# Gate/up units of four FFNs as seven half-width products, with one weight sum made by transfers

## The chip, the core and the metric

The kernel runs on one core of one Trainium2 chip. The metric is the device time of one execution in microseconds (us): from three runs of the kernel before, the median is 2486.27 us (2479.25 to 2486.68). TensorE is called PE, VectorE DVE, ScalarE ACT, GpSimd POOL; SP is the engine that issues most of the loads.

## What is computed

Two transformer blocks over 512 positions of width 1024, batch 1, all in 32-bit floats: pooling with grid attention, an mLSTM, HGRN2 beside stick-breaking attention, a cross-attention to a memory of 256 rows, and four feed-forward parts. The change touches only the four feed-forward parts:

```python
FFN_HIDDEN = 2816
def swiglu(h, w1, w3, w2):                # ffn0 and ffn1
    return (jax.nn.silu(h @ w1) * (h @ w3)) @ w2
def swiglu_2(h, w_gu, w_down):            # ffn2 and ffn3
    gu = h @ w_gu
    gate, up = jnp.split(gu, 2, axis=-1)
    return (jax.nn.silu(gate) * up) @ w_down
# x = x + g2 * swiglu(h, w1, w3, w2)      or      x = x + 0.5 * swiglu_2(rmsnorm(x), w_gu, w_down)
```

## The kernel before

**Layout.** Activations stand with features on the 128 partitions: `x`, `h_hi`, `h_lo` are 8 chunks (KC) of 128 features x 512 positions. Weights come from HBM as `stream`, one unit of 128 x 2048 floats (1 MB) after the other, into `raw`, which has two slots (unit m uses slot m % 2).

**Three passes.** To keep the precision of 32 bits, each operand is split in a rounded high part and the rest: for weights ACT writes `w_hi` (`split_hi`, L214) and DVE `w_lo` (`split_lo`, L218). Each product is three matmuls: hi x hi, hi x lo, lo x hi (`three_passes`, L231 to L233).

**An FFN** (`FeedForward`) has 22 gate/up units (FB) and 11 down units. A gate/up unit holds 128 columns of the gate and 128 of the up weights, each over 8 chunks: 2 x 8 x 3 = 48 matmuls of 512 columns, into two PSUM banks. ACT takes the silu of the gate bank (L717), or of the copy that DVE scaled first (L747, L749, then L714) where the norm is deferred (ffn2 and ffn3: the matmuls begin on x times gain, and the row factors `inv_rows` are applied to the results). DVE multiplies by the up half (L754), ACT writes `g_hi` (L719) and DVE `g_lo` (L756). Then `split_next_hi` and `split_next_lo` split the weights two units ahead. The 22 chunks of g stay in SBUF. A down unit is 2 chunks of g x 8 output blocks x 3 passes, again 48 matmuls of 512 columns; all eight banks accumulate over the 11 units, and DVE adds the result to x (L786) as the banks of the last unit end.

**Queues.** Each engine runs its own list in order; waits are on semaphores. SP loads unit m as soon as the split of unit m - 2 is done (`lo_split`, L2796). POOL issues most loads of the conditioning weights (`load_ada`, L2788, 48 units of 1 MB in all, 13 of them by SP), of which DVE adds up 8 in the gate/up units of ffn0 and 16 in its down units (`Conditioning.add_unit`, L326). In ffn0, the norm before it and ffn1's are of the plain kind (`Norm`), in which DVE scales x chunk by chunk, ACT writes `h_hi` and DVE `h_lo`.

## Time and profile before

| | |
|---|---|
| median of 3 runs | 2486.27 us (2479.25 to 2486.68) |
| profiled execution, span from first to last instruction | 2481.9 us |
| four FFNs, matmuls of 512 columns | 4 x 33 x 48 = 6336 of 12256 |
| HBM read | 263.90 MB, 107 GB/s over the span |

Durations below come from the one profiled execution. Its span of 2481.9 us is within the three runs and 4.4 us under their median. In the profile a line like L218 is that of a helper, so one line stands for all its uses; the shapes tell them apart. Matmuls are pipelined: the duration of one is longer than the distance from one to the next, and it is the distance that counts. Where a row tells of idle time before a group of instructions, the releaser is the instruction that ended the wait.

### The profile page before, as it was taken

The page shows a single profiled execution, that of the slowest core. Times are in us where ns is not written, and L with a number is a line of the kernel's source. Part 1 is how long each engine was busy: PE and PEld are TensorE (multiplying, and loading weights), DVE is VectorE, ACT ScalarE, POOL GpSimd, SP SyncE. Part 2 cuts the span into 40 slices and gives each one's busy share as a digit, 9 for nine tenths or more (in the row PEclk, how much of TensorE's full clock was granted, in tenths as well). Part 3 has the DMA queues.
Part 4 walks back from the last instruction along what each step waited for, and adds up shares of the span by engine and source line. Part 5 has one row for each costly group of instructions (what it writes and reads, how often), then busy time and mean ns, then how long its engine had stood idle before and what let it go on. Part 6 is the DMA issues. An engine that isn't in the chain of part 4 may idle for free.

```text
span 2481.9 us, 30237 instructions
## 1 busy us (share of the span) xinstructions
PE 2416.7 (97%) x12256; PEld 2022.5 (81%) x12256; DVE 1238.3 (50%) x1449; ACT 902.1 (36%) x1215; POOL 70.3 (3%) x81
## 2 busy tenths in 40 slices
PE   7989999999999999999999999999999999999998
PEld 6658888888799778888878888879989877888886
DVE  6677543356746543332254442346678545444423
ACT  3353333313344333332143332244556544333311
POOL 0210000000003000000000000000000000000000
PEclk9999999999999999999999999999999999999999
DMA  8116522364233122222222222221212212222221
GB/s 341 73 63 243 186 102 101 139 239 164 87 123 91 68 84 86 101 101 100 87 85 101 98 88 102 102 98 69 85 52 79 75 68 85 85 101 101 88 100 67
DMA packets 40549, 267.34 MB, mean 108 GB/s; under 512 B 4394, under 2 KB 5674, under 8 KB 9490
## 3 DMA queue, kind: packets, MB, share of 16 engines
q1 hardware_dynamic: 31248, 219.87, 24.6%
q0 software_dynamic: 5840, 40.37, 4.2%
q10 hardware_dynamic: 3378, 5.91, 0.9%
q8 instruction: 61, 1.00, 0.2%
q14 instruction: 22, 0.18, 0.0%
HBM read 263.90 MB, written 2.24 MB: 107 GB/s over the span
## 4 chain that ended last, share of the span: by engine, by line
PE 89%; DVE 6%; ACT 3%; issue 1%; DMA 0%; DVEq 0%; SPq 0%; ACTq 0%
PE bank L231 26%; PE bank L233 26%; PE bank L232 26%; DVE w_lo L218 1%; PE bank L2160 1%; ACT w_hi L214 1%; PE bank L2256 1%; PE bank L334 1%; PE bank L2243 1%; PE bank L1868 1%; DVE work L461 1%; DVE work L445 1%; PE bank L2231 1%; PE bank L1864 1%; ACT work L438 1%
## 5 line engine op out<-in xcount | busy, mean ns | idle before, releaser
L231 PE MATMUL bank<-h_hi,w_hi 128*128 128x512 f32 x1800 | 711.1, 395 | 5.3 <-DVE w_lo L218 2.0
L233 PE MATMUL bank<-h_hi,w_lo 128*128 128x512 f32 x1800 | 703.3, 391 | 0.0
L232 PE MATMUL bank<-h_lo,w_hi 128*128 128x512 f32 x1800 | 703.3, 391 | 0.0
L218 DVE TENSOR_TENSOR w_lo<-raw,w_hi 128x2048 fp32r<-128x2048 f32 x192 | 439.9, 2291 | 477.6 <-ACT w_hi L214 477.6
L214 ACT ACTIVATE w_hi<-raw 128x2048 fp32r<-128x2048 f32 x192 | 366.3, 1908 | 413.1 <-PE bank L233 409.6
L231 PEld LDWEIGHTS bank<-h_hi,w_hi 128*128 128x128 f32 x1800 | 339.5, 189 | 82.0 <-issue 6.7
L233 PEld LDWEIGHTS bank<-h_hi,w_lo 128*128 128x128 f32 x1800 | 339.4, 189 | 71.8
L232 PEld LDWEIGHTS bank<-h_lo,w_hi 128*128 128x128 f32 x1800 | 339.7, 189 | 70.6 <-issue 1.4
L233 PE MATMUL bank<-g_hi,w_lo 128*128 (+1 forms) x704 | 273.9, 389 | 0.0
L231 PE MATMUL bank<-g_hi,w_hi 128*128 (+1 forms) x704 | 273.9, 389 | 0.0
L232 PE MATMUL bank<-g_lo,w_hi 128*128 (+1 forms) x704 | 273.9, 389 | 0.0
L231 PEld LDWEIGHTS bank<-g_hi,w_hi 128*128 128x128 f32 x704 | 132.1, 188 | 27.5
L232 PEld LDWEIGHTS bank<-g_lo,w_hi 128*128 128x128 f32 x704 | 132.1, 188 | 27.5
L233 PEld LDWEIGHTS bank<-g_hi,w_lo 128*128 128x128 f32 x704 | 132.1, 188 | 27.3
L754 DVE TENSOR_TENSOR work<-work,bank 128x512 f32<-128x512 f32 x44 | 30.2, 688 | 212.5 <-ACT work L717 212.5
L231 PE MATMUL bank<-w_hi,h_hi 128*128 128x256 f32 x448 | 130.4, 291 | 2.0 <-DVE w_lo L218 2.0
L232 PE MATMUL bank<-w_lo,h_hi 128*128 128x256 f32 x448 | 127.3, 284 | 0.0
L233 PE MATMUL bank<-w_hi,h_lo 128*128 128x256 f32 x448 | 127.2, 284 | 0.0
L717 ACT ACTIVATE work<-bank 128x512 f32<-128x512 f32 x44 | 26.3, 598 | 277.0 <-PE bank L233 274.9
L714 ACT ACTIVATE work<-work 128x512 f32<-128x512 f32 x44 | 27.8, 632 | 262.6 <-DVE work L747 262.6
L747 DVE TENSOR_TENSOR work<-bank,inv_rows 128x512 f32<-128x512 f32 x44 | 30.4, 692 | 165.8 <-PE bank L233 160.5
L756 DVE TENSOR_TENSOR g_lo<-work,g_hi 128x512 f32 (+1 forms) x88 | 61.0, 693 | 79.0 <-ACT g_hi L719 79.0
(331 smaller groups left out, 2816.9 us busy)
## 6 DMA issues: line engine op xcount, KB each, us to landing
raw<-stream SPq DMA_DIRECT2D x192, 1024.0 KB, 4.8
work<-stream POOLq DMA_DIRECT2D x19, 1024.0 KB, 6.5
h_plain<-stream POOLq DMA_DIRECT2D x16, 1024.0 KB, 5.4
work<-stream SPq DMA_DIRECT2D x13, 1024.0 KB, 12.3
work<-mlstm_rows ACTq DMA_DIRECT2D x8, 512.0 KB, 4.8
x<-xT SPq DMA_DIRECT2D x1, 2048.0 KB, 10.5
outT<-work SPq DMA_DIRECT2D x8, 256.0 KB, 2.3
work<-mlstm_rows ACTq DMA_DIRECT2D x8, 192.0 KB
```

Source lines behind the costliest of these rows:

```text
L214: nc.scalar.activation(w_hi[:, slot(m), :], raw[:, slot(m), :], ACT.Copy).then_inc(hi_split, 1)
L218: nc.vector.tensor_tensor(w_lo[:, slot(m), :], raw[:, slot(m), :], w_hi[:, slot(m), :], ALU.subtract).then_inc(lo_split, 1)
L231: nc.tensor.matmul(out, stationary[0], moving[0], start=first, stop=False)
L232: nc.tensor.matmul(out, stationary[0], moving[1], start=False, stop=False)
L233: return nc.tensor.matmul(out, stationary[1], moving[0], start=False, stop=last)
L334: last = nc.tensor.matmul(bank[:, self.banks[a], 16 * q + b:16 * q + b + 1], self.acc[a][:, b * P:b * P + P], ones[:, 0:1], start=True, st ...
L438: nc.scalar.activation(self.sq[:, k, :], x[:, k, :], ACT.Square).then_inc(sq_done, 1)
L714: nc.scalar.activation(self.silu[:, r, :], self.silu[:, r, :], ACT.Silu).then_inc(silu_done, 1)
L717: nc.scalar.activation(self.silu[:, r, :], bank[:, b, :], ACT.Silu).then_inc(silu_done, 1)
L747: nc.vector.tensor_tensor(self.silu[:, r, :], bank[:, b, :], inv_rows[:, :], ALU.mult).then_inc(rows_scaled, 1)
L754: nc.vector.tensor_tensor(self.gu[:, r, :], self.silu[:, r, :], up, ALU.mult).then_inc(gated, 1)
L756: nc.vector.tensor_tensor(g_lo[:, bass.ds(2 * i + r, 1), :], self.gu[:, r:r + 1, :], g_hi[:, bass.ds(2 * i + r, 1), :], ALU.subtract).then ...
```

## The change

Of the 22 gate/up units of each FFN the first 4 (`FFN_WHOLE`) stay as they are. The other 18 (`FAST`) compute the same 2 x 2 block product with seven products instead of eight. The unit's output is seen as gate and up rows x first and second 256 positions, the inner dimension as even and odd chunks. A product is then 4 chunks x 3 passes of 256 columns, and there are seven: 84 matmuls of 256 columns in place of 48 of 512.

- **Weights.** The host stores a fast unit as four parts of 512 columns: a12, a11, a22 and a fourth (`parts` in `ffn_units`). Four more blocks are sums of them. s3 and s1 are made by a transfer of POOL that accumulates parts 2 and 3 on a copy of parts 1 and 2 (`mixes`, 0.25 MB + 0.25 MB). s2 = s3 + a22 is made by DVE (`make_further`). s4, the sum of all four, is made by POOL: a plain transfer of part 0 into `further`, then a transfer that accumulates s2 on it (`add_further`).
- **Activations.** POOL forms five differences of quarters of h (`gpsimd`), in a deferred stage after eight multiplications by the gain; ACT and DVE split the result (`hidden_high`, `hidden_low`).
- **Results.** ACT copies the first product (`keep_first`), DVE makes three additions (`add_first`) and a last one (`add_last`); then silu and gating (`apply`, `gate_chunk`).
- **Splits.** A fast unit is split in three pieces instead of one: three plain blocks (`whole_high`, `whole_low`), two mixes, two further blocks. The chunks of g are kept whole and split in pairs beside the down units (`pair_high`, `pair_low`).
- **Loads.** SP issues three transfers for a fast unit (parts 0 and 1, part 3, parts 1 and 2). The loops over units on all engines are written out. The down weights wait until `further`, which lies in the fourth quarter of both `raw` slots, is free.
- Some semaphores are merged (`set_loaded`, `act_prepared`, `dve_prepared`), and the rings of the conditioning loads in ffn0 move.

The core of the diff:

```diff
+FFN_WHOLE = 4
+            mixes = [area(4096, UNIT // 2), area(5120, UNIT // 2)]
+            further = raw[:, :, 3 * (UNIT // 4):]
+            def load(self, sp, m):
+                q, r, s = self.QUARTER, m - self.fast(0), slot(m)
+                sp.wait_ge(lo_split, m - 1)
+                src = stream[place_of(m), :, :]
+                sp.dma_start(raw[:, s, 0:2 * q], src[:, 0:2 * q]).then_inc(landed[s], 16)
+                sp.dma_start(raw[:, s, 2 * q:3 * q], src[:, 3 * q:]).then_inc(landed[s], 16)
+                sp.wait_ge(part_lo, self.hidden_lows(2) if r < 2 else self.part_low("mixes", r - 2))
+                sp.dma_start(self.mixes[s], src[:, q:3 * q]).then_inc(landed[s], 16)
+            def add_parts(self, pool, r):
+                q, s = self.QUARTER, slot(self.fast(r))
+                pool.wait_ge(landed[s], landings(self.fast(r)))
+                pool.dma_start(self.mixes[s], stream[place_of(self.fast(r)), :, 2 * q:], accum_op=ALU.add).then_inc(
+                    mixed_in[s], 16)
+            def add_further(self, pool, r):
+                if r:
+                    pool.wait_ge(part_lo, self.part_low("further", r - 1))
+                else:
+                    pool.wait_ge(lo_split, self.fast(0))
+                pool.dma_start(self.further[:, 1, :], stream[place_of(self.fast(r)), :, 0:self.QUARTER]).then_inc(further_in, 16)
+                pool.wait_ge(further_in, 32 * (self.w0 + r) + 16)
+                pool.wait_ge(part_lo, self.part_low("s2", r))
+                pool.dma_start(self.further[:, 1, :], self.further[:, 0, :], accum_op=ALU.add).then_inc(further_in, 16)
+            def gpsimd(self, pool):
...
+                for i, (out, one, two) in enumerate(((b11, b12, b11), (b12, b22, b12), (b21, b22, b21), (b22, b11, b22),
+                                                     (b21, b21, b11))):
+                    nc.gpsimd.tensor_tensor(out, one, two, ALU.subtract).then_inc(hidden_sums, 1)
+                    pool.wait_ge(hidden_sums, self.sums_base + self.sums_first + i + 1)
...
+                self.add_parts(pool, 0)
+                for r in range(FAST):
+                    if r + 1 < FAST:
+                        self.add_parts(pool, r + 1)
+                    self.add_further(pool, r)
+            def make_further(self, dve, r):
+                nc.vector.tensor_tensor(s2, s3, a22, ALU.add).then_inc(part_lo, 1)
+            def further_high(self, act, r):
+                act.wait_ge(further_in, 32 * (self.w0 + r + 1))
+                act.wait_ge(unit_used, self.fast(r))
+                nc.scalar.activation(out, self.further, ACT.Copy).then_inc(part_hi, 1)
+            # ACT, fast units
+                for r in range(FAST):
+                    self.further_high(act, r)
+                    if r:
+                        self.apply(act, r - 1)
+                    if r + 1 < FAST:
+                        self.whole_high(act, r + 1)
+                    self.keep_first(act, r)
+                    if r + 1 < FAST:
+                        self.mixes_high(act, r + 1)
+            # DVE, fast units
+                for r in range(FAST):
+                    self.further_low(dve, r)
+                    if r:
+                        self.add_last(dve, r - 1)
+                    if r + 1 < FAST:
+                        self.make_further(dve, r + 1)
+                    if r:
+                        self.gate_chunk(dve, r - 1)
+                    if r + 1 < FAST:
+                        self.whole_low(dve, r + 1)
+                        self.mixes_low(dve, r + 1)
...
+                    self.add_first(dve, r)
+                    if self.ada and r and r % 2 == 0 and r < 16:
+                        conditioning.add_unit(dve, 3 * KC + r // 2)
+            # PE, fast units: 3, 2 and 2 products of 4 chunks x 3 passes x 256 columns
+            def plain_products(self, pe, r):
+                pe.wait_ge(lo_split, self.fast(r) + 1)
...
+            def mixes_products(self, pe, r):
+                pe.wait_ge(part_lo, self.part_low("mixes", r))
...
+            def further_products(self, pe, r):
+                pe.wait_ge(part_lo, self.part_low("further", r))
...
+                    if m == ffn.md or m == ffn.md + 1:
+                        sp.wait_ge(part_lo, ffn.part_low("further", FAST - 1))
```

## Rows read from the trace of the kernel before

**Rows 1.** The page: busy time by engine, and the chain that ended last.
```profile
PE 2416.7 (97%) x12256; PEld 2022.5 (81%) x12256; DVE 1238.3 (50%) x1449; ACT 902.1 (36%) x1215; POOL 70.3 (3%) x81
PE 89%; DVE 6%; ACT 3%; issue 1%; DMA 0%; DVEq 0%; SPq 0%; ACTq 0%
```

**Rows 2.** Windows: stretches inside the FFNs; the last beside POOL's conditioning loads.
```profile
core 0: us, PE busy (x) PEld busy (x) DVE busy (x) ACT busy (x) POOL busy (x), PEclk, DMA share, GB/s
...
338.00:468.00 130.00, 130.00 (x585) 108.00 (x584) 42.05 (x37) 42.44 (x41) 0.00 (x0) 0.99 0.26 93
905.00:1035.00 130.00, 130.00 (x575) 107.66 (x574) 43.67 (x36) 44.16 (x42) 0.00 (x0) 1.00 0.27 96
1295.00:1425.00 130.00, 130.00 (x576) 107.63 (x575) 59.60 (x60) 44.56 (x42) 0.00 (x0) 1.00 0.28 96
...
1120.00:1150.00 30.00, 30.00 (x134) 24.85 (x133) 8.26 (x5) 6.05 (x6) 0.00 (x0) 1.00 0.30 105
540.00:600.00 60.00, 60.00 (x266) 49.67 (x266) 36.33 (x17) 11.50 (x6) 3.70 (x7) 1.00 0.62 235
```

**Rows 3.** Groups by line, 1295 to 1425 us, DVE and ACT (x12 is 12 units).
```profile
L218 DVE TENSOR_TENSOR w_lo<-raw,w_hi 128x2048 fp32r<-128x2048 f32 x12 | 27.5, 2293 | 11.7 <-ACT w_hi L214 11.7
L747 DVE TENSOR_TENSOR work<-bank,inv_rows 128x512 f32<-128x512 f32 x12 | 8.3, 692 | 46.5 <-PE bank L233 46.5
...
L214 ACT ACTIVATE w_hi<-raw 128x2048 fp32r<-128x2048 f32 x12 | 22.8, 1900 | 0.0
...
L719 ACT ACTIVATE g_hi<-work 128x512 f32 x12 | 7.6, 633 | 10.6 <-DVE work L754 10.6
```

**Rows 4.** Timeline of DVE in the down stage of ffn1 (start us, us, instruction).
```profile
1194.48 2.29 DVE L218 TENSOR_TENSOR w_lo<-raw,w_hi 128x2048 fp32r<-128x2048 f32 x1 [8.64 <-ACT w_hi L214]
1205.30 2.29 DVE L218 TENSOR_TENSOR w_lo<-raw,w_hi 128x2048 fp32r<-128x2048 f32 x1 [8.53 <-ACT w_hi L214]
1216.24 2.29 DVE L218 TENSOR_TENSOR w_lo<-raw,w_hi 128x2048 fp32r<-128x2048 f32 x1 [8.64 <-ACT w_hi L214]
1227.06 2.29 DVE L218 TENSOR_TENSOR w_lo<-raw,w_hi 128x2048 fp32r<-128x2048 f32 x1 [8.53 <-ACT w_hi L214]
1237.94 2.29 DVE L218 TENSOR_TENSOR w_lo<-raw,w_hi 128x2048 fp32r<-128x2048 f32 x1 [8.59 <-ACT w_hi L214]
```

**Rows 5.** Timeline of ACT in the odd input stage, where units are 256-column matmuls.
```profile
701.06 1.21 ACT L1481 ACTIVATE work<-bank 128x256 f32<-128x256 f32 x4 [8.51 <-PE bank L233]
...
712.58 1.21 ACT L1481 ACTIVATE work<-bank 128x256 f32<-128x256 f32 x4 [2.02 <-PE bank L233]
```

**Rows 6.** Windows: the odd input stage around those units.
```profile
680.00:720.00 40.00, 40.00 (x337) 40.00 (x336) 22.10 (x30) 15.49 (x25) 5.13 (x4) 1.00 0.39 125
```

**Rows 7.** Groups of the whole span: fused DVE kinds, gate update of 512, conditioning of 2048.
```profile
L326 DVE SCALAR_TENSOR_TENSOR work<-work,cond 128x2048 f32<-128x2048 f32 x28 | 65.8, 2348 | 9.5 <-DMA work<-stream 8.6
...
L786 DVE SCALAR_TENSOR_TENSOR x<-bank,par,x 128x512 f32<-128x512 f32 x16 | 11.8, 748 | 9.2 <-PE bank L233 9.1
```

**Rows 8.** DMA issues (median us from issue to landing), and POOL's issues themselves.
```profile
raw<-stream SPq DMA_DIRECT2D x192, 1024.0 KB, 4.8
...
outT<-work SPq DMA_DIRECT2D x8, 256.0 KB, 2.3
...
work<-mix_tables POOLq DMA_DIRECT2D x1, 768.0 KB, 4.6
...
L2788 POOL DMA_DIRECT2D work<-stream x19: 527/527/599, 51.0 to 315.8; - x19
```

**Rows 9.** POOL's additions: duration min/median/max ns, and their group.
```profile
L1581 POOL TENSOR_TENSOR work<-work,tab x16: 1262/1296/3071, 694.7 to 798.8; 128x512 f32<-128x512 f32 x16
...
L1581 POOL TENSOR_TENSOR work<-work,tab 128x512 f32<-128x512 f32 x16 | 24.7, 1564 | 194.9 <-DMA work<-mlstm_rows 194.9
```

**Rows 10.** Windows: the tail of ffn1 and the start of ffn2.
```profile
1240.00:1265.00 25.00, 22.95 (x100) 18.11 (x99) 18.46 (x27) 13.86 (x21) 0.00 (x0) 0.93 0.21 75
```

More of the change, by code:

```diff
@@ new lines, in whole_high, with whole_low @@
+            def whole_high(self, act, r):
+                m = self.fast(r)
+                act.wait_ge(landed[slot(m)], landings(m))
+                if r:
+                    act.wait_ge(products, self.product_done(4, r - 1))
+                else:
+                    act.wait_ge(unit_used, m - 1)
+                nc.scalar.activation(self.weights(0, 3)[0], raw[:, slot(m), 0:3 * self.QUARTER], ACT.Copy).then_inc(hi_split, 1)
+            def whole_low(self, dve, r):
+                m = self.fast(r)
+                dve.wait_ge(hi_split, m + 1)
+                hi, lo = self.weights(0, 3)
+                nc.vector.tensor_tensor(lo, raw[:, slot(m), 0:3 * self.QUARTER], hi, ALU.subtract).then_inc(lo_split, 1)
@@ L839, in rows @@
-                def rows(d, i, first=False, end=False):
-                    m = self.md + d
+                    if j == 0 and self.norm.deferred:
+                        self.norm.spread_row(pe)
+                pe.wait_ge(part_lo, self.hidden_lows(2))
+                for r in range(FAST):
+                    self.plain_products(pe, r)
+                    self.mixes_products(pe, r)
+                    self.further_products(pe, r)
+                    if self.ada and r == 15:
+                        conditioning.sum_rows(pe, 3)
```

542 lines of the change are left out of this document (385 added, 157 removed).

## The prediction

> **What bounds the kernel now.** I read the busy table and the chain that ended last first: TensorE (PE) is busy 97% of the span and carries 89% of the chain; VectorE (DVE) is busy 50%, ScalarE (ACT) 36%, GpSimd (POOL) 3% [rows 1]. Then the stretches inside the gate/up stages of the four FFNs: PE is busy for the whole of each, DVE for 42 to 60 of 130 us, the DMA engines for 0.26 to 0.28 of their time at 93 to 96 GB/s, and the granted clock is 0.99 to 1.00, so TensorE runs at its upper level of 2.4 GHz [rows 2]. Nothing but matmul time limits these stages: DVE waits for PE's banks and for ACT (46.5 us before L747 in one stretch) [rows 3]. So removed matmul work is worth its full time, until something else takes longer per unit. A unit, gate/up or down, is 48 matmuls of 512 columns. The DVE splits of five successive weights of a down stage start 10.82 to 10.94 us apart (43.46 us for four, mean 10.87): 226 ns a matmul [rows 4].
>
> **What a fast unit costs on PE.** Of the 22 gate/up units of each FFN, 18 become seven products of 4 chunks x 3 passes: 84 matmuls of 256 columns. If time went by columns alone, that would be 84/96. The row for 256 columns is in the odd input stage: a unit of 96 such matmuls is evacuated at 701.06 and the next at 712.58, 11.52 us, 120 ns each [rows 5]; there the weight load is busy in all of 40.00 us, so the load, not the column count, sets that pace [rows 6]. 84 x 0.120 = 10.08 us against 10.87: 0.79 us saved per unit, 72 units, 57 us. The ceiling is therefore 2481.9 - 57 = 2425 us.
> The Trainium skill (TensorE: Matmul & The Clock Gate, Back-to-back issue gap) gives a warm isolated gap of columns/2.4 + 2.5 ns. By it a unit would go from 10.36 to 9.17 us and 72 units would save 86 us. The rows show a smaller gain and decide.
>
> **DVE and ACT in a fast unit.** DVE takes 0.69 us for 512 columns and 2.29 for 2048 [rows 3], hence 0.16 + 1.04 per 1000 columns: 0.42 at 256, 1.22 at 1024, 1.76 at 1536. Per unit: low parts 1.76 + 1.22 + 1.22; `make_further`, two of `add_first` and `add_last` 4 x 0.69; the third add 0.42; the gating 0.75 (the fused kind, [rows 7]). Sum 8.1, and 8.8 where the norm is deferred (one more 0.69). It was 3.7 and 5.0. That is under 10.08, but no longer hidden by half an engine of slack: the order of the queue now matters. In ffn0 nine conditioning additions of 2.35 [rows 7] add 1.2 per unit: 9.3. ACT: 0.63 at 512 and 1.90 at 2048 [rows 3] give 1.06 + 1.48 + 1.06 + 0.63 + 0.4 = 4.6, no bound.
>
> **The transfers, the step that decides.** The stream per unit was one 1 MB load. Now it is 1.25 MB by SP (parts 0-1, part 3, then parts 1-2 again into `mixes`), and three POOL transfers: 0.5 MB accumulated into `mixes`, 0.25 MB plain into `further`, and 0.25 MB accumulated there from SBUF. The last two form a chain that goes through every unit, since `further` is one buffer: `further_low`(r-1) on DVE, POOL issues the plain one, waits until it has landed, issues the accumulating one, ACT `further_high`, DVE `further_low`(r). Prices: a plain 0.25 MB takes 2.3 us from issue to landing, 1 MB 4.8, hence 1.5 + 3.3 per MB; POOL's 0.75 MB took 4.6 where this gives 4.0, so 0.5 more on POOL (its issue alone is 0.53) [rows 8]. Plain into `further`: 2.8.
> No row shows an accumulating transfer. Below, it costs what a plain one of its size does; I see no reason for a saving under that. It must read its destination as well as its source and write the sum, so the nearest row is a transfer of twice its bytes, which I take: 0.25 MB for 1.5 + 0.5 + 1.65 = 3.6 us, and 0.5 MB of it occupies the queue for 3.3 us. Above, I take three times the bytes.
> The chain then is 2.8 + 3.6 + 1.06 + 1.22 + 0.3 for the hand-overs (five at about 0.06) = 9.0 us. Alone it would fit under 10.08. But POOL issues `add_parts`(r+1), 0.5 MB accumulating, just before the plain transfer of `add_further`(r), in the same queue. Its source `mixes` is free only after `mixes_low`(r-1), its reload takes about 3.2 us and shares the engines, so it goes out about when `further_low`(r-1) ends, and the plain transfer stands behind it. Of its 3.3 us of service I count 2.8 on the chain: period 11.8 us. With a price like a plain one it is 8.2 + 1.4 = 9.6, under PE's 10.08; with three times the bytes 9.9 + 4.2 = 14.1.
> Why PE must follow: on DVE `whole_low`(r+1) is queued behind `further_low`(r), `add_last`, `make_further` and the gating (4.6 to 5.3 us after it), and `plain_products`(r+1) waits for it; `further_products`(r) waits for the chain itself. The engines move 2.25 MB, as I price it the work of 3 MB, in 11.8 us, 254 GB/s; 235 GB/s took a share of 0.62 [rows 2], so bandwidth is not exceeded, but transfers will meet each other.
> The Trainium skill (DMA: Bandwidth & Descriptors, Anatomy of one DMA) gives 2.0 us + bytes/436e3 per POOL transfer: 2.6 us for 0.25 MB, near the row's. By it the chain with both transfers at that price is 7.8 us and the change would reach PE's floor. It says nothing of an accumulating transfer, and the sum keeps the rows.
>
> **Entry and exit.** Entry: POOL forms five differences of 1024 columns per partition; its 512-column rows last 1.27 to 1.56 us [rows 9], so 12.5 to 15.6. They start when h is complete, some 10.5 us after its first chunk (two fused DVE steps of 0.75 for each of seven more, [rows 7]); then come 5 us of ACT and 4 of DVE: 32 to 35 us. The silu of unit 1 is queued behind them on ACT, and unit 3, due at 32.6 or later, needs it. 0 to 3 us each; I take 1, four times: 4. In deferred stages POOL's eight gains also run beside DVE's x updates at the tail of the stage before, where PE already idles 2.05 of 25 us [rows 10]; 0 to 3 us, in the same 4. Exit: the down weights of the first pair can load only after the last `further_low`, since `further` lies in `raw`: 4.8 + 1.90 + 2.29 [rows 3, 8] = 9.0 us to the first down matmul. The last unit's products cover about 5.5 of it: 3.5 lost, four times 14. Before there was no such wait: PE is busy for the 30 us around the turn [rows 2]. In the down stage g is split in pairs: 1.06 ACT, 2.4 DVE beside 10.87 of PE, hidden by PE, at most 2 x 2.35 more in ffn0 (9.4 in all). The renamed semaphores and SP's unrolled loads cost nothing: they stand off PE's path.
>
> **Sum.** -57 (matmuls), + 72 x (11.8 - 10.08) = +124 (chain), -16 (in the first two to three units of each stage the chain has a lead, about 4 us each), +4, +14: 2481.9 + 69 = 2551. The median lies 4 us above the profiled span: 2555 us, 2.8% slower.
>
> **The rivals, and how the numbers follow.** The time is 2447 + 72 x (period - 10.08), less up to 16 for the lead.
> A, the forecast: the chain through `further` sets a period of 11 to 13 us. For it: the in-order queues as written, and two landings one after the other per unit. Chance 0.50, 2505 to 2625.
> B, the accumulating transfer costs like a plain one: the chain stays under 10.08, only entry and exit remain: 2481.9 - 57 + 18 + 4 = 2447, faster. It decides at a period of 10.6: above it the chain has eaten 72 x 0.5 = 36 us of the 57, entry and exit the rest. For it: fixed latency (1.5 of 2.3) is most of a small transfer, and a source in SBUF may be quicker. Chance 0.20.
> C, in between, 1.25 to 1.5 times: period 10.4 to 11.1, 2470 to 2512, within 1%. Chance 0.17.
> D, the accumulating transfers are three times or more, or the stalls (2 us and more per unit) also lower TensorE's clock: where PE idled at the tail above, the granted clock was 0.93 [rows 10]. Period 13 and up, 2640 and more. Chance 0.10.
> E, DVE becomes the bound instead: its 8.8 us grow if POOL and DVE hold each other up (one POOL row of 512 columns took 3.07 us against 1.27 [rows 9]). From 10.08 on it decides; at 10.6 the result is about 2485. Chance 0.03.
> Range: 2445 to 2640 leaves out most of D and little else. This kernel's measurement tells about 0.3% (7 us) from no change. Faster: B and a fifth of C, 0.23; same: 0.07; slower: 0.70.
>
> **What would show it.** PE idle of 1.5 to 2 us before the matmuls of `plain_products` and `further_products`, ended by DVE's `w_lo` writes; ACT's `further_high` waiting for a DMA; POOL waiting most of its time between the two transfers. Right if their starts lie 11 to 13 us apart, accumulating landings take 3 to 4 us (5 for 0.5 MB), and DVE is idle 2 us or more per unit. Wrong if the period is 10.1 and PE has no gaps (B), if DVE is busy without a gap (E), or if a 256-column matmul with weights as the stationary side is not 120 ns: at 113 ns the ceiling falls by 42 us, but the chain would hide that.

## The result, and the profile after

The changed kernel takes 2718.18 us (median of 4 runs, 2713.82 to 2724.46) against 2486.47 us for the kernel before on the same chip: a ratio of 1.0949 (95% interval 1.0931 to 1.0967; the two medians alone give 1.0932). The forecast was 2555, with a range up to 2640: right in its direction, but the loss is 232 us where 69 were expected.

The page of the changed kernel answers to rows 1 (busy time, queues, chain) and rows 8 (landings).

```profile
span 2716.4 us, 35297 instructions
PE 2452.1 (90%) x14848; PEld 2170.9 (80%) x14848; DVE 1612.4 (59%) x1913; ACT 989.8 (36%) x1369; POOL 327.7 (12%) x333
...
q0 software_dynamic: 32336, 115.88, 18.5%
...
PE 53%; DMA 23%; DVE 11%; ACT 7%; issue 4%; POOL 2%; SPq 0%; ACTq 0%; DVEq 0%; POOLq 0%
...
work<-stream SPq DMA_DIRECT2D x72, 512.0 KB, 6.1
work<-stream POOLq DMA_DIRECT2D x72, 512.0 KB, 5.7
...
raw<-stream POOLq DMA_DIRECT2D x72, 256.0 KB, 4.1
raw<-raw POOLq DMA_DIRECT2D x72, 256.0 KB, 4.6
```

PE fell from 97% busy to 90%, and from 89% of the chain to 53%; transfers, absent from the chain before, carry 23%. The last four lines are, in order, SP's reload of `mixes`, POOL's accumulation on it, the plain transfer into `further` and the accumulating one. L240, L960 and the other line numbers from here on are those of the changed kernel (L240 is a matmul, L960 is the difference in `further_low`, L922 that in `whole_low`, L937 that in `mixes_low`).

The waits (engine and line, what ended the wait, us in total, times, longest):

```profile
ACT w_hi L955 <- DMA raw<-raw: 479.3, 71, 12.2
POOL work L817 <- DMA work<-stream: 431.0, 72, 21.6
...
POOL raw L829 <- DMA raw<-stream: 311.5, 71, 7.6
...
PE bank L240 <- DVE w_lo L960: 133.2, 40, 6.4
...
PE bank L240 <- DVE w_lo L922: 32.8, 30, 2.0
```

ACT waits for the accumulated sum in 71 of 72 units. PE waits behind it in only 40, about every second one, but then 3.3 us in the mean.

Windows answer to rows 2: four long ones inside the fast units of ffn0 to ffn3, three short ones in ffn2 ahead of them, and last the turn from gate/up to down units in ffn1.

```profile
core 0: us, PE busy (x) PEld busy (x) DVE busy (x) ACT busy (x) POOL busy (x), PEclk, DMA share, GB/s
...
1500.00:1515.00 15.00, 13.61 (x114) 13.41 (x112) 7.89 (x10) 3.84 (x5) 3.16 (x4) 1.00 0.72 207
1515.00:1523.00 8.00, 5.39 (x33) 5.10 (x34) 6.72 (x8) 3.66 (x5) 1.44 (x2) 0.79 0.58 120
...
1541.00:1547.00 6.00, 4.40 (x24) 4.24 (x24) 4.87 (x6) 3.39 (x5) 1.16 (x2) 0.72 0.52 117
...
290.00:490.00 200.00, 158.76 (x1180) 154.63 (x1178) 120.53 (x130) 60.81 (x71) 34.98 (x47) 0.90 0.71 190
990.00:1200.00 210.00, 173.28 (x1221) 165.97 (x1220) 110.97 (x131) 62.94 (x76) 34.03 (x44) 0.91 0.68 169
1440.00:1640.00 200.00, 169.77 (x1284) 166.41 (x1283) 126.71 (x150) 65.50 (x76) 34.57 (x45) 0.93 0.70 181
2360.00:2560.00 200.00, 161.44 (x1227) 158.38 (x1228) 126.66 (x151) 65.50 (x76) 34.54 (x45) 0.93 0.69 173
...
1255.00:1270.00 15.00, 10.54 (x37) 8.35 (x36) 9.06 (x9) 5.29 (x4) 0.00 (x0) 0.77 0.38 129
```

Where the kernel before had the clock at 0.99 to 1.00 and the DMA engines at 0.26 to 0.28, the clock is now 0.90 to 0.93 and the engines are at 0.68 to 0.71. The loss of clock is not spread evenly: it is 1.00 in a stretch without a gap, and 0.72 to 0.79 in the short stretches in which PE has just stood idle for some 3 us. A closer look at one such place, the first matmul behind a wait and the 3 us after it:

```profile
1490.92 0.57 PE L240 MATMUL bank<-t_hi_tile,w_hi 128*128 128x256 f32 x1 [3.47 <-DVE w_lo L960]
```

```profile
1491.00:1494.00 3.00, 3.00 (x14) 3.00 (x15) 2.45 (x4) 1.78 (x2) 0.57 (x1) 0.50 0.75 179
```

The granted clock is 0.50 there, the lower level of 1.2 GHz, and the matmuls start 0.21 us apart; from 1494.45 on they start 0.12 us apart again.

**Where the 232 us lie.** Each FFN is taken from the start of DVE's last run of x updates before it (for ffn2, which follows ffn1 directly, from ffn1's first update) to its own first update. The four FFNs took 1448.1 us before and 1680.7 after: all of the loss. By stages (timelines of PE and DVE, the four summed; before, the 18 units are 18 x 10.87, rows 4):

| us, four FFNs | before | after | difference |
|---|---|---|---|
| entry and the 4 whole units | 215.2 | 229.6 | +14.4 |
| 18 fast units and the wait behind them | 782.7 | 990.9 | +208.2 |
| down units | 450.0 | 460.2 | +10.2 |

Of the 990.9 us, 72 x 10.08 = 726 are matmuls at the forecast pace, 166 are PE's waits for L960 and L922 (133.2 + 32.8), 17.7 the four waits at the exits (6.9 and 10.8). What is left, 81 us, is time above the forecast pace. The clock windows account for most of it: at a mean clock of about 0.92, the 807 us in which PE works take 807 x (1 - 0.92) = 65 us more than at 1.00. PE's timelines say it directly: 608 of the 6048 matmuls start 0.21 or 0.22 us after the one before, the pace of the lower level, and cost 57 us more than at 0.120. Some 12 us more lie at the 75 waits, where idle time counts only from the end of the last matmul, and 4 are 32 small matmuls of the conditioning, which the table's column for the kernel before has in its first row.

**One turn of the loop.** The timelines of SP, POOL and DVE in ffn2 (start us, us, instruction, idle time before it and what ended it) show what sets the pace:

```profile
1523.02 0.37 SPq L811 DMA_DIRECT2D work<-stream  x1
```

```profile
1517.00 0.57 POOL L826 DMA_DIRECT2D raw<-stream  x1 [2.87 <-DVE w_lo L960]
1520.55 0.87 POOL L829 DMA_DIRECT2D raw<-raw  x1 [2.99 <-DMA raw<-stream]
1528.74 0.88 POOL L817 DMA_DIRECT2D work<-stream  x1 [7.32 <-DMA work<-stream]
1529.28 0.91 POOL L826 DMA_DIRECT2D raw<-stream  x1
1535.50 0.86 POOL L829 DMA_DIRECT2D raw<-raw  x1 [5.32 <-DMA raw<-stream]
```

```profile
1499.48 1.22 DVE L960 TENSOR_TENSOR w_lo<-raw,w_hi 128x1024 fp32r<-128x1024 f32 x1 [0.55 <-ACT w_hi L955]
...
1515.47 1.22 DVE L960 TENSOR_TENSOR w_lo<-raw,w_hi 128x1024 fp32r<-128x1024 f32 x1 [6.70 <-ACT w_hi L955]
...
1521.77 1.22 DVE L937 TENSOR_TENSOR w_lo<-work,w_hi 128x1024 fp32r<-128x1024 f32 x1
...
1525.21 1.23 DVE L960 TENSOR_TENSOR w_lo<-raw,w_hi 128x1024 fp32r<-128x1024 f32 x1 [0.44 <-ACT w_hi L955]
...
1541.32 1.22 DVE L960 TENSOR_TENSOR w_lo<-raw,w_hi 128x1024 fp32r<-128x1024 f32 x1 [6.82 <-ACT w_hi L955]
```

L960 starts 16.0 us after the last time, then 9.7, then 16.1: not every unit is slow, every second one is. From 1515.47: `whole_low` and `mixes_low` stand behind `further_low` in DVE's queue, so L937 ends only at 1522.99; that frees `mixes`, and SP starts its reload at 1523.02, 7.55 us after L960 began; POOL, next in its queue `add_parts` of that later unit (L817), waits until the reload has landed, to 1528.74 (5.72); only then does it issue the plain transfer of `add_further` (L826), whose buffer had been free since 1526.4; that one shares the engines with the 0.5 MB just issued and lands after 6.2 us (1535.50); the accumulating transfer, ACT and the hand-overs take 5.8. The sum is 7.55 + 5.72 + 0.54 + 6.22 + 5.82 = 25.85 us, for two units: 12.9 each. The means of the 17 steps in ffn2 and ffn3 are 12.8 and 13.0. The short step between is the chain through the one buffer without anything in its way: L960 at 1515.47, L826 at 1517.00, L829 at 1520.55, L960 again at 1525.21, 9.7 us where the forecast had 9.0.

### The profile page after: what moved, and what is told of

It is laid out like the page before. It is cut to its first block, busy times and chain, and to the rows that moved or that the text cites. A ratio compares the mean times of both kernels' runs of the same rounds, so it can differ in the third digit from the quotient of the medians.

```text
span 2716.4 us, 35297 instructions
## 1 busy us (share of the span) xinstructions
PE 2452.1 (90%) x14848; PEld 2170.9 (80%) x14848; DVE 1612.4 (59%) x1913; ACT 989.8 (36%) x1369; POOL 327.7 (12%) x333
## 3 DMA queue, kind: packets, MB, share of 16 engines
q0 software_dynamic: 32336, 115.88, 18.5%
## 4 chain that ended last, share of the span: by engine, by line
PE 53%; DMA 23%; DVE 11%; ACT 7%; issue 4%; POOL 2%; SPq 0%; ACTq 0%; DVEq 0%; POOLq 0%
PE bank L240 14%; PE bank L241 14%; PE bank L242 14%; DMA raw<-stream 8%; DMA work<-stream 7%; DMA raw<-raw 7%; ACT w_hi L916 2%; DVE w_lo L922 1%; ACT w_hi L955 1%; DVE w_lo L937 1%; POOL work L846 1%; DVE w_lo L227 1%; PE bank L343 1%; ACT w_hi L223 1%; PE bank L2554 1%
## 5 line engine op out<-in xcount | busy, mean ns | idle before, releaser
L240 PE MATMUL bank<-h_hi,w_hi 128*128 128x256 f32 (+1 forms) x1512 | 528.7, 350 | 44.9 <-DVE w_lo L922 32.8
L241 PE MATMUL bank<-h_lo,w_hi 128*128 128x256 f32 (+1 forms) x1512 | 515.0, 341 | 0.0
L242 PE MATMUL bank<-h_hi,w_lo 128*128 128x256 f32 (+1 forms) x1512 | 513.4, 340 | 0.0
L240 PE MATMUL bank<-t_hi_tile,w_hi 128*128 128x256 f32 x1152 | 343.4, 298 | 133.4 <-DVE w_lo L960 133.2
L240 PEld LDWEIGHTS bank<-h_hi,w_hi 128*128 128x128 f32 x1512 | 306.3, 203 | 85.7 <-DVE w_lo L922 39.7
L227 DVE TENSOR_TENSOR w_lo<-raw,w_hi 128x2048 fp32r<-128x2048 f32 x120 | 279.4, 2328 | 147.5 <-ACT w_hi L223 147.5
L240 PEld LDWEIGHTS bank<-t_hi_tile,w_hi 128*128 128x128 f32 x1152 | 232.2, 202 | 141.9 <-DVE w_lo L960 141.7
L242 PE MATMUL bank<-t_hi_tile,w_lo 128*128 128x256 f32 x1152 | 338.4, 294 | 0.0
L241 PE MATMUL bank<-t_lo_tile,w_hi 128*128 128x256 f32 x1152 | 338.1, 294 | 0.0
L240 PE MATMUL bank<-g_hi,w_hi 128*128 128x512 f32 x704 | 278.5, 396 | 18.1 <-DVE w_lo L227 10.8
L241 PE MATMUL bank<-g_lo,w_hi 128*128 128x512 f32 x704 | 277.1, 394 | 0.0
L242 PE MATMUL bank<-g_hi,w_lo 128*128 128x512 f32 x704 | 277.0, 393 | 0.0
L960 DVE TENSOR_TENSOR w_lo<-raw,w_hi 128x1024 fp32r<-128x1024 f32 x72 | 88.2, 1225 | 299.1 <-ACT w_hi L955 298.8
L242 PEld LDWEIGHTS bank<-t_hi_tile,w_lo 128*128 128x128 f32 x1152 | 233.7, 203 | 0.0
L240 PEld LDWEIGHTS bank<-g_hi,w_hi 128*128 128x128 f32 x704 | 134.3, 191 | 47.9 <-DVE w_lo L227 11.4
```

The costliest lines, as they stand in the source:

```text
L227: nc.vector.tensor_tensor(w_lo[:, slot(m), :], raw[:, slot(m), :], w_hi[:, slot(m), :], ALU.subtract).then_inc(lo_split, 1)
L240: nc.tensor.matmul(out, stationary[0], moving[0], start=first, stop=False)
L241: nc.tensor.matmul(out, stationary[0], moving[1], start=False, stop=False)
L242: return nc.tensor.matmul(out, stationary[1], moving[0], start=False, stop=last)
L960: nc.vector.tensor_tensor(lo, self.further, hi, ALU.subtract).then_inc(part_lo, 1)
```

## The experiments

Line numbers are those of each kernel; L960 and L976 are `further_low`.

### The sum of four blocks by DVE

```diff
                 nc.vector.tensor_tensor(s2, s3, a22, ALU.add).then_inc(part_lo, 1)
+                dve.wait_ge(part_lo, self.part_low("s2", r))
+                nc.vector.tensor_tensor(self.further[:, 1, :], s2, raw[:, s, 0:q], ALU.add).then_inc(part_lo, 1)
...
-                    self.add_further(pool, r)
```

> One part undone: the sum of all four blocks is a DVE addition of 512 columns again (0.69 us a unit), POOL's plain and accumulating transfers through the buffer further are gone, the accumulation into mixes stays. Theory Q (the queue theory: units are paced by the chain of landings through further, lengthened by POOL's order, in which the plain transfer stands behind the accumulation for the next unit; the starts of the low part of further alternate between 9.8 and 16 us, 12.9 on the mean in ffn2): the alternation goes, the period falls to 10.1 to 11 us, total 2470 to 2540 us. Rival V (DVE's in-order queue paces): 0.69 us more on DVE per unit, the period stays at 13 or rises, total 2700 to 2770 us. Rival B (the DMA engines are short of time, share 0.70): 0.5 of 2.25 MB less per unit, the period falls by a fifth, to 10.5 to 11.5, but the landings of mixes stay at 6 us.

2500.89 us, ratio 1.0071 (1.0053 to 1.0088). One addition of 0.69 us on DVE in place of the two transfers wins back 217 of the 232 us. Starts of `further_low` (here L961) in ffn1:

```profile
1025.46 1.22 DVE L961 TENSOR_TENSOR w_lo<-raw,w_hi 128x1024 fp32r<-128x1024 f32 x1
...
1035.54 1.22 DVE L961 TENSOR_TENSOR w_lo<-raw,w_hi 128x1024 fp32r<-128x1024 f32 x1
```

They are 10.08 us apart, the forecast's floor for PE, 84 x 0.120. So the pace of 120 ns for 256 columns [rows 5] carried over to weights of another shape, and in ffn1 the rest of the change, accumulating `mixes` included, fits under it (mean 10.1). In ffn2 and ffn3 the starts scatter (7.9 to 13.4 us) round means of 10.3 and 10.2, and in all DVE waits 28 times, 71.9 us, for an accumulation into `mixes`; only a part of that reaches PE. That the kernel still does not gain has other places. PE waits 15.2 us for `whole_low` and 19.9 for the splits of whole weights (L227), and ffn0 takes 384.2 us against 369.6 before.

### POOL issues the further sums first

```diff
                 for r in range(FAST):
+                    self.add_further(pool, r)
                     if r + 1 < FAST:
                         self.add_parts(pool, r + 1)
-                    self.add_further(pool, r)
```

> Same work, one order changed: POOL issues both transfers of further for unit r before the accumulation into mixes for unit r+1. Theory Q: the plain transfer is no longer behind the 0.5 MB accumulation, it lands 3.5 us after its issue every time (before 3.5 and 6.5 in turn), period 10.8 to 11.8, total 2560 to 2640 us. Rivals V and B: DVE's work and the bytes are the same, total stays within 15 us of 2718.

2669.69 us, ratio 1.0755 (1.0725 to 1.0786), 48 us less than the change, between the two ranges that I had given. The period is now irregular (9.5 to 17 us in ffn1 to ffn3), and the landings of the transfers for `mixes` are longer: 9.3 and 9.8 us instead of 6.1 and 5.7. That they now meet the chain through `further` is my explanation; no run shows it. The order costs something, but it is not the whole.

### Both accumulating transfers made plain

This kernel moves the same bytes and leaves the sums out.

```diff
-                pool.dma_start(self.mixes[s], stream[place_of(self.fast(r)), :, 2 * q:], accum_op=ALU.add).then_inc(
+                pool.dma_start(self.mixes[s], stream[place_of(self.fast(r)), :, 2 * q:]).then_inc(
...
-                pool.dma_start(self.further[:, 1, :], self.further[:, 0, :], accum_op=ALU.add).then_inc(further_in, 16)
+                pool.dma_start(self.further[:, 1, :], self.further[:, 0, :]).then_inc(further_in, 16)
```

> Both accumulating transfers are made plain ones of the same size and place, so the sums of the weight blocks are left out. It prices the accumulation. If an accumulation costs as much as twice its bytes (as I priced it), the landing of the 0.5 MB falls from 5.7 to about 4.2 us and that of the 0.25 MB from 4.6 to about 3.7; theory Q: 2.5 to 4 us less per two units, total 2580 to 2630 us. Rival B: share of the DMA engines falls from 0.70 to 0.55, period 10.5 or less, total under 2530. If the accumulation is nearly free: within 20 us of 2718.

2632.27 us, ratio 1.0581 (1.0557 to 1.0604): 86 us less, at the upper end of what I had expected. The bytes are the same (115.88 MB in the queue), the time is not:

```profile
q0 software_dynamic: 27728, 115.88, 12.8%
...
work<-stream POOLq DMA_DIRECT2D x72, 512.0 KB, 4.1
...
raw<-raw POOLq DMA_DIRECT2D x72, 256.0 KB, 2.8
```

The addition lengthens a landing of 512 KB from 4.1 to 5.7 us and one of 256 KB from 2.8 to 4.6. But 144 us of the loss (0.0581 x 2486) stay with plain copies, in the same pattern (in ffn2 9.2, then 15 to 16 us). A cheap accumulation would not have made the change pay: the loop alone loses.

### The sums of `mixes` by POOL's adder as well

On top of the first experiment, `add_parts` becomes two POOL additions of 512 columns; no accumulating transfer is left.

```diff
+                nc.gpsimd.tensor_tensor(m[:, 0:q], m[:, 0:q], m[:, q:], ALU.add).then_inc(mixed_in[s], 1)
+                pool.wait_ge(mixed_in[s], self.mixes_in(r) - 1)
+                nc.gpsimd.tensor_tensor(m[:, q:], m[:, q:], raw[:, s, 2 * q:3 * q], ALU.add).then_inc(mixed_in[s], 1)
```

> As e1_sum_on_dve, and the two sums of mixes are made by two POOL additions of 512 columns (about 1.3 to 1.6 us each) in place of the accumulating transfer: no accumulating transfer is left, 1.25 MB in three plain transfers per unit remain. Theory Q: period at PE's floor of 10.1 us but for DVE's queue, total 2445 to 2490 us. Rival V: no better than e1_sum_on_dve. If POOL and DVE hold each other up at SBUF, DVE's additions of 512 columns from SBUF get longer than 0.69 us and the total is over that of e1_sum_on_dve.

2530.73 us, ratio 1.0179 (1.0155 to 1.0202): 30 us slower than with the accumulating transfer and above the 2445 to 2490 that I had expected, with period 11.2 us in ffn2 and ffn3 (10.4 in ffn1). The timelines of POOL and DVE over a unit and the next show why:

```profile
1502.78 1.29 POOL L818 TENSOR_TENSOR work<-work 128x512 f32<-128x512 f32 x1 [8.93 <-DMA work<-stream]
1504.15 2.69 POOL L820 TENSOR_TENSOR work<-work,raw 128x512 f32<-128x512 f32 x1
```

```profile
1502.92 2.77 DVE L923 TENSOR_TENSOR w_lo<-raw,w_hi 128x1536 fp32r<-128x1536 f32 x1
1505.61 2.32 DVE L938 TENSOR_TENSOR w_lo<-work,w_hi 128x1024 fp32r<-128x1024 f32 x1
...
1514.24 1.76 DVE L923 TENSOR_TENSOR w_lo<-raw,w_hi 128x1536 fp32r<-128x1536 f32 x1
1515.92 1.22 DVE L938 TENSOR_TENSOR w_lo<-work,w_hi 128x1024 fp32r<-128x1024 f32 x1
```

While POOL adds (1502.8 to 1506.8), DVE's two differences take 1.0 and 1.1 us more than in the next unit, where POOL is silent; POOL's own second addition takes 2.69 where its first took 1.29. The four end in turn, POOL at 1504.07, DVE at 1505.69, POOL at 1506.84, DVE at 1507.93. DVE has no idle time from 1499.4 to 1514.1, longer than a whole unit, so what it loses to POOL here lengthens the period. This is the forecast's rival E, in the kernel where it decides. An accumulating transfer does have a use: it keeps such a sum off both engines.

### Two buffers for the further sums

In ffn1 to ffn3 `further` alternates between two buffers; the plain transfer waits for `further_low`(r-2) instead of (r-1).

```diff
+            def further(self, r):
+                return area(7168, 2, UNIT // 4) if r % 2 and not self.ada else self.shared
...
+            def before_further(self, eng, r):
+                back = r - (1 if self.ada else 2)
+                if back >= 0:
+                    eng.wait_ge(part_lo, self.part_low("further", back))
...
```

> The changed kernel, but the further sums of ffn1, ffn2 and ffn3 alternate between two buffers, so that the plain transfer of a unit waits for the difference two units back and not for the last one; GpSimd's order is that of the changed kernel, and so are all bytes. Chain theory (the time is set by a chain over two units that runs through the one buffer: difference, VectorE's queue, reload of the sums 6.1 us, its GpSimd accumulation, the plain transfer behind it 6.2, the accumulating one 3.6, ScalarE and VectorE 2.3): without the one buffer the chain opens, the starts of the difference L960 come every 10.1 to 11 us in ffn2 and ffn3 instead of 12.9 to 13.1, the clock there rises from 0.90 to above 0.95, and the time is 2718 less about 54 units of 2.3 us less some 45 us of clock: 2550, 2520 to 2590. Bandwidth theory (the DMA engines, 0.70 busy at 13 us per unit, would have to be 0.88 busy at 10.3, and landings grow before that): the period stays above 12 us, landings of the 256 KB accumulation grow beyond 5 us, and the time stays above 2660. Queue theory (VectorE's and GpSimd's order is what counts, not the buffer): the period hardly moves, with landings unchanged, above 2660 too.

2707.52 us, ratio 1.0902 (1.0873 to 1.0932). The chain theory as I had put it there fell: with the one buffer gone, 11 us come back, not 170. POOL and DVE in ffn2:

```profile
1493.06 0.88 POOL L836 DMA_DIRECT2D work<-stream  x1 [7.80 <-DMA work<-stream]
1494.37 0.57 POOL L843 DMA_DIRECT2D work<-stream  x1 [0.44 <-issue]
```

```profile
1479.50 1.23 DVE L976 TENSOR_TENSOR w_lo<-work,w_hi 128x1024 fp32r<-128x1024 f32 x1 [7.14 <-ACT w_hi L971]
1489.04 1.23 DVE L976 TENSOR_TENSOR w_lo<-raw,w_hi 128x1024 fp32r<-128x1024 f32 x1 [0.26 <-ACT w_hi L971]
1505.74 1.23 DVE L976 TENSOR_TENSOR w_lo<-work,w_hi 128x1024 fp32r<-128x1024 f32 x1 [7.39 <-ACT w_hi L971]
```

The plain transfer (L843) is free of its buffer, and is still issued only after POOL's 7.80 us for the reload; the long period is 16.7 us where it was 16.0 to 17.7. The turn of the loop above goes through two in-order queues, DVE's (`mixes_low` behind `further_low`) and POOL's (`add_further` behind `add_parts`), not through the buffer.

### Two buffers, and the further sums first

```diff
                 for r in range(FAST):
+                    self.add_further(pool, r)
                     if r + 1 < FAST:
                         self.add_parts(pool, r + 1)
-                    self.add_further(pool, r)
```

> The two buffers, and besides it GpSimd issues the further sums of a unit before the accumulation of the next unit's other sums, so that nothing of the further sums is queued behind the reload. Chain theory: the reload no longer stands in the path of the further sums at all; if the two buffers alone have opened the chain, this one changes little (within 30 us of the two-buffer run); if GpSimd's wait for the reload still holds the plain transfer, it is faster than that run by more than 30 us, near 2540. Bandwidth theory: both stay above 2660, and the landing of the reload or of the accumulation is longer than 6 us in the median.

2611.99 us, ratio 1.0515 (1.0497 to 1.0532): 96 us less than the two buffers alone, though not the 2540 that I had expected. Together the two edits bring 106 us, singly 48 and 11: each opens one of two paths into the same transfer. The period in ffn1 to ffn3 falls to 11.5 us in the mean, and the clock there rises to 0.97 to 0.98. The long step is now the path of `mixes`: its reload lands in 9.3 us and its accumulation in 9.2 (`DMA work<-stream` is 18% of the chain), and with 1.06 of ACT, 1.22 of DVE and 0.3 of hand-overs that is 21.1 us for a slot that comes round every two units: by this estimate 10.5 each before any wait in the engines' own queues, over PE's 10.08.

### The same, with plain copies

Here too the sums are left out.

```diff
-                pool.dma_start(self.mixes[s], stream[place_of(self.fast(r)), :, 2 * q:], accum_op=ALU.add).then_inc(
+                pool.dma_start(self.mixes[s], stream[place_of(self.fast(r)), :, 2 * q:]).then_inc(
...
-                pool.dma_start(self.further(r)[:, 1, :], self.further(r)[:, 0, :], accum_op=ALU.add).then_inc(further_in, 16)
+                pool.dma_start(self.further(r)[:, 1, :], self.further(r)[:, 0, :]).then_inc(further_in, 16)
```

> The kernel with two buffers and the further sums issued first, and both accumulating transfers made plain (as many bytes, but nothing is added: the sums of blocks are left out and the output is wrong for it). What remains between that kernel (2612) and the one with the sum on VectorE (2501) is 111 us. Theory: most of what remains is the price of the accumulating transfers on busy DMA engines (share 0.77 to 0.80 there, landings of 9 us); plain ones land in 4 to 6 us, the period falls from 11.5 to 10.3 to 10.8, and the time is 2560, 2530 to 2580. Rival (the bytes and the order of the queues are what remains, not the addition): the landings stay near 9 us, and the time stays above 2595.

2506.65 us, ratio 1.0095 (1.0074 to 1.0116): 105 us less, more than expected, and level with the sum on DVE. `further_low` starts every 10.1 us through ffn1 to ffn3, but for the first one or two steps; only ffn0, which has no second buffer here, is irregular (405.5 us against 384.2 with the sum on DVE). The queue and the same window in ffn1, first with the accumulating transfers, then with plain ones:

```profile
q0 software_dynamic: 32336, 115.88, 18.4%
...
990.00:1200.00 210.00, 187.08 (x1452) 181.97 (x1452) 132.07 (x156) 77.86 (x86) 41.07 (x53) 0.98 0.80 198
```

```profile
q0 software_dynamic: 27728, 115.88, 13.4%
...
990.00:1200.00 210.00, 206.38 (x1551) 198.49 (x1551) 141.87 (x158) 85.51 (x90) 23.92 (x45) 1.00 0.59 198
```

At the same 198 GB/s the engines are busy 0.80 of the time with accumulation and 0.59 without (the second window reaches 44 us into the down units, which end sooner there; over the fast units of ffn1 alone it is 0.79 at 199 GB/s against 0.66 at 221). In engine time: 18.4% of 2614.0 us is 481 us, 13.4% of 2504.4 is 336; the 145 us between them are 2.0 us of all 16 engines per unit for 0.79 MB accumulated. The same 0.79 MB plain take 336 / 115.88 x 0.79 = 2.3, so an accumulated byte costs 1.9 times a plain one. The same sum for the changed kernel and its plain copies gives 2.0.

So there are two prices, the order of the waits and the accumulation, and they nearly add up: 108 and 92 us singly, 212 together. The table gives the loss against the kernel before, from ratios times 2486 (hence 236 and not 232):

| | accumulating | plain copies |
|---|---|---|
| POOL's order of the change, one buffer | 236 | 144 |
| further sums first, one buffer | 188 | not run |
| order of the change, two buffers | 224 | not run |
| further sums first, two buffers | 128 | 24 |
| sum on DVE | 18 | |

### The differences of ffn2 late

On top of the first experiment, POOL's five differences of h in ffn2 wait for the scale of the norm.

```diff
+                    if not self.norm.squares_added:
+                        pool.wait_ge(inv_done, self.norm.n + 1)
```

> The kernel with the sum of all four blocks made by VectorE, and in ffn2's entry GpSimd's five differences wait until the norm's scale is ready. Theory of the shared memory port (VectorE's seven additions of squares took 13.5 us instead of 5.5 because GpSimd's 13.6 us of differences ran beside them): the additions take 5.5 to 7 us again, ffn2's entry is 5 to 8 us shorter, and the time is 2494, 2490 to 2498, against 2501. Rival (the additions wait on their inputs, or on ScalarE's squares): they take over 12 us again, and the time is 2500 or above, since the differences come later.

2497.45 us, ratio 1.0054 (1.0037 to 1.0071). DVE's seven additions of squares in ffn2's entry, first with the differences beside them, then without:

```profile
1264.33 13.52 DVE L454 TENSOR_TENSOR work<-work 128x512 f32<-128x512 f32 x7
```

```profile
1273.06 5.68 DVE L454 TENSOR_TENSOR work<-work 128x512 f32<-128x512 f32 x7
```

13.52 against 5.68 us (5.47 in the kernel before), and ffn2 takes 361.9 us instead of 370.7. Its entry, up to the first fast unit, is 58.7 us instead of 65.3 (56.5 in the kernel before). That settles most of the entry's loss in ffn2: two-input subtractions of POOL beside two-input additions of DVE. The total fell by only 3 us, inside the scatter of the two kernels' runs: ffn0, which the edit leaves alone, took 393.4 us in this profiled execution and 384.2 in the other.

### ffn0 as before

On top of the first experiment, ffn0 is the `FeedForward` of the kernel before: 22 whole units and its rings for the conditioning loads.

```diff
-            for name in ("ffn0", "ffn1", "ffn2", "ffn3"):
+            for name in ("ffn1", "ffn2", "ffn3"):
...
+        class WholeFeedForward:
```

> The kernel with the sum of all four blocks made by VectorE, with ffn0 computed as in the kernel before (22 whole units): one of the three edits of the combined kernel (2471). By the sum of stages ffn0 goes from 384 to 370 us and nothing else moves: 2487, 2482 to 2492. Rival (the combined kernel's gain came from the split load and the late differences, and ffn0 as it is costs nothing): 2496 to 2501.

2478.34 us, ratio 0.9972 (0.9959 to 0.9984): for the first time under the kernel before, and below the 2482 to 2492 that I had expected. By the profiled spans, ffn0 gives back 16.4 us (384.2 to 367.8) of 17.0; between the medians the gain is 22.6, since the profiled execution of the first experiment was its fastest. There the seven products save matmuls too, but DVE has the conditioning additions: in the first experiment it is busy 161.0 us of the 200 from 290 on, 9.0 us per unit at a mean period of 11.2. That this is what costs ffn0 its gain is a reading; no run shows it apart.

### ffn0 as before, late differences, down weights in two pieces

```diff
+                        for n in (m, m + 1):
+                            sp.dma_start(raw[:, slot(n), 0:c], stream[place_of(n), :, 0:c]).then_inc(landed[slot(n)], 16)
...
+                        for n in (m, m + 1):
+                            sp.dma_start(raw[:, slot(n), c:], stream[place_of(n), :, c:]).then_inc(landed[slot(n)], 16)
```

> The kernel of the run before with two more edits: ffn0 is computed as in the kernel before (22 whole units, no products of sums), and the down weights of the first pair are loaded in two pieces, three quarters before and one quarter after the last difference of the further sums. By the sum of stages: ffn0 went from 384 back to 370 us (-14); the port wait -7; the exits of three feed-forwards from about 4 us of idle TensorE to about 1 (-9): 2501 - 30 = 2471, 2460 to 2485, below the 2486 of the kernel before. Rival (each such stall only moves: a later load meets the next one): 2490 to 2505.

2471.12 us, ratio 0.9952 (0.9936 to 0.9969), 12 us under the kernel before: the fastest of the study. The total is as expected, but not for all of the expected reasons. PE's wait at ffn2's exit is 3.14 us with the split load and 3.14 without: it gained nothing there. The late differences cut PE's wait for the norm in ffn2 from 9.75 to 1.89 us, but 3.24 us of it come back at once as a wait for a weight's low part, and four waits of 0.6 to 2.5 us follow in the fast units where there were two, of 0.9 and 1.8; ffn2 as a whole is 1.4 us shorter. Most of the gain over the first experiment, 25 of 30 us by the ratios, is ffn0. That the two other edits gain anything was not told apart: the intervals of the two kernels overlap.

## Why the prediction was wrong

**Right.** The floor of PE, 10.08 us per unit (10.08 and 10.1 in the kernels whose transfers keep up). The Trainium skill (TensorE: Matmul & The Clock Gate, Back-to-back issue gap) would have given 9.17; the runs decide for the row. The place: the transfers of `further`, in two landings one after the other, with the plain one queued behind the 0.5 MB; without them 217 us come back. The price of an accumulated byte in engine time, forecast as twice a plain one: 1.9. A free landing of 0.25 MB accumulated, forecast 3.6 us: 3.6 in the median of the loop's stretch. The exits of ffn1 to ffn3, forecast 10.5 us: 10.8. That all four come near the forecast's 14 (17.7) is luck: ffn0's 6.9 us are a wait for the conditioning's `write_mod` (L353), which the forecast did not have. Of the signs in the trace, ACT's `further_high` waits for a DMA, POOL waits between its two transfers, and PE is idle before `plain_products` and `further_products`; but the starts are 13.5 us apart and not 11 to 13, and the accumulating landings take 4.6 and 5.7 us and not 3 to 4 and 5.

**The step that failed** is the one that puts the chain at 9.0 + 2.8 = 11.8 us and closes it over one unit. It says of the reload of `mixes` that it "takes about 3.2 us and shares the engines, so it goes out about when `further_low`(r-1) ends", and prices the wait as 2.8 us of service. Two things were wrong with it.

- *The loop was cut short.* I had noted that `whole_low` is queued behind `further_low` on DVE, and that `add_parts` waits for the reload, but I did not join the two: `further_low` delays `mixes_low`, that the reload, that `add_parts`, and that `further_low` two units on. In each second unit POOL stands 7.3 us at L817, and L826 with it. The path is 25.85 us for two units, and it took the second buffer and POOL's other order together for 106 us to come back. The two queues were as plain in the diff as the buffer; the two-buffer run shows that the buffer, on which I had built the chain, was worth 11 us.
- *Landings were priced as if alone.* The reload took 5.7 to 6.1 us, not 3.2; the plain transfer 4.1 in the median and 6.2 to 6.5 in the slow units, not 2.8; the last 0.25 MB 4.6 in the median, not 3.6. With the forecast's own prices in the two-unit path the sum is 7.55 + 3.2 + 0.54 + (2.8 + 2.8) + (3.6 + 1.36) = 21.9, or 10.9 per unit: by the right path and lone landings the forecast would have been still lower than its 11.8. The other 4.0 us of the 25.85 are the landings' excess over these prices. The engines were 0.70 busy; I had written that bandwidth was not exceeded and that "transfers will meet each other", and gave the meeting no price. With two buffers and POOL's other order, taking the accumulation away brings the landings of `mixes` from 9.2 and 9.3 to 4.5 and 5.9 us and makes the kernel 105 us faster, so the landings' price under load is not small.

**The size of the loss.** The mean period over all 72 units is 990.9 less 17.7, divided by 72: 13.52 us, not 11.8. That is 72 x 1.72 = 124 us; the lead of 16 us did not appear: the first period in ffn2 is already 14 us. The exits cost 4 more and the entries 10 more than forecast (ffn2's additions of squares, above), the down units 10, to which I had put nothing: at the turn in ffn1 the clock is 0.77 (last window above), and PE's timelines have 46 matmuls of 512 columns right behind the four exits that start some 0.43 us apart instead of 0.226, 9.4 us in all. 124 + 16 + 4 + 10 + 10 = 164, to rounding which is the gap between 2555 and 2718. Two slips in the sums changed nothing: by the forecast's own formula a period of 13 us is 2641 and not the 2625 of A's upper end, and 3 MB of units in 11.8 us are 267 GB/s and not 254.

**The clock.** It belongs inside those 13.5 us: behind the gaps of 3 us in every second unit it falls to the lower level, 57 us by the matmuls' distances and 65 by the windows. Where the gaps go, so does the loss: in ffn1 to ffn3 of the kernel with plain copies, two buffers and the other order no matmul of the fast units starts 0.21 us after another. The forecast had the clock only in rival D, at a chance of 0.10, though 2 us of gap per unit were part of rival A itself: with A's gaps, the clock's fall was a term of the sum and not a case of its own.

**The rivals.** B and C (an accumulation at the price of a plain transfer, or at 1.25 to 1.5 times it) are refuted twice: the landings differ, and with plain copies the loss is still 144 us. The Trainium skill (DMA: Bandwidth & Descriptors, Anatomy of one DMA) gives 2.6 us for 0.25 MB; here the plain one took 3.2 at the least and 4.1 in the median. E did not happen in this kernel (DVE is 0.53 to 0.63 busy in the windows of the fast units), but its mechanism is real: it took 8 us in ffn2's entry, and it stands behind the 30 us that POOL's additions cost in the kernel that has them. D named the right total, from one right cause of its two: the price of accumulation is not three times, the clock did fall.

**Left open.** How much of ffn0's loss in the changed kernel (442.1 us, the largest of the four) is the conditioning loads in the shared queue and how much DVE's additions: no run separates them. Of the 81 us above the forecast pace some 8 have no place, and no experiment changed the clock by itself. The 4.0 us by which the landings on the path exceed their prices were not split between the accumulation and the other transfers.

## What to carry to other kernels

A chain of waits must be followed until it comes back to the instruction it began with, through every in-order queue on the way and over as many iterations as there are buffers; a step that "goes out about when" another ends is where the loop hides. Price a landing at the load that the changed kernel will have, not at that of the kernel before, and if the forecast puts gaps in TensorE's work, put the lower clock in the same sum. To replace a 0.7 us addition by two dependent transfers cost 217 us here, though the engine had room for it: with the addition on it, DVE was busy 124.4 us of 160 in ffn1, 2.2 us idle per unit. Even with two buffers, POOL's other order and nothing added, the transfers only drew level with it; an accumulating transfer pays where two iterations of slack lie behind it, as for `mixes` here.

## What the runs showed of the hardware

- An accumulating transfer cost 1.9 to 2.0 times the engine time of a plain one per byte. Landings in the median: 5.7 against 4.1 us for 512 KB from HBM, 4.6 against 2.8 for 256 KB within SBUF (at the least 3.3 against 2.2).
- With the further sums issued first and two buffers, the 512 KB landings into `mixes` (POOL's, and SP's reload) took 9.2 and 9.3 us with accumulation (engines 0.75 to 0.79 busy in the fast units of ffn1 to ffn3), 4.5 and 5.9 with plain copies (0.63 to 0.66).
- Behind a wait of 3.47 us TensorE's granted clock was 0.50, with 256-column matmuls 0.21 us apart, and 1.00 in the stretches between, with 0.12 us; so its mean of 0.90 to 0.93 is a mixture of its two levels (1.2 and 2.4 GHz).
- Two-input operations on GpSimd and VectorE at once hold each other up: of the seven 512-column additions of VectorE in ffn2's entry, the four beside GpSimd's subtractions took 2.64 to 2.68 us where an undisturbed one takes 0.69, and GpSimd's second addition took 2.69 against 1.29. The Trainium skill (SBUF — State Buffer, "SBUF: two separate sides") says that the two engines share a pair of ports, and that where VectorE's operation has two inputs in SBUF and GpSimd's reads SBUF, the one that starts first holds the pair to its end. The trace agrees: in the kernel with POOL's additions the two engines' operations end one after the other, 1.1 to 1.6 us apart.
